# The MLP of a four-layer hybrid backbone: x spilled and fetched in pieces, the tenth pair's weights in the modulation buffers, the last modulation part in the layer's own MLP

## The reference

```python
m = silu(c) @ mod_w[i] + mod_b[i]            # six parts of 1024: m[0] to m[5]
...                                          # mixer with m[0], m[1], m[2]
h = rmsnorm(x, g4[2]) * (1.0 + m[4]) + m[3]
f = square(relu(h @ mlp_w1[i])) @ mlp_w2[i]  # 1024 -> 4096 -> 1024
x = x + m[5] * rmsnorm(f, g4[3])
```

## Time and profile before

| | us |
|---|---|
| median of 3 runs | 3561.32 (3553.54 to 3561.75) |
| the profiled execution | 3556.74 |
| its span | 3554.9 |
| PE busy | 3209.8 (90%) |
| PE weight load busy | 2971.0 (84%) |
| DVE busy | 2062.0 (58%) |
| POOL busy | 1944.1 (55%) |
| ACT busy | 1481.6 (42%) |
| mean granted TensorE clock | 0.961 of full |

### The profile page before, as it was taken

The page is one execution under the profiler, slowest core; times in us unless marked ns, Lnnn a source line. Parts: engine busy times, 40 slices in busy tenths (PEclk is TensorE's granted clock), DMA queues, the critical chain, the costliest instruction groups (busy, mean ns, idle before and its releaser), DMA issues.

```text
span 3554.9 us, 73409 instructions
## 1 busy us (share of the span) xinstructions
PE 3209.8 (90%) x28786; PEld 2971.0 (84%) x28786; DVE 2062.0 (58%) x3756; ACT 1481.6 (42%) x2812; POOL 1944.1 (55%) x1467
## 2 busy tenths in 40 slices
PE   5899998999999998898688889899988989999997
PEld 2789998899889997796577788899987856889996
DVE  8646884564558854859844444478735643543333
ACT  4344433422544444546432234444435343544442
POOL 0455676554556774525577744557764301556674
PEclk9899999999999998998799999999999999999999
DMA  7445553333355533336734433455533201342214
GB/s 283 160 148 186 199 196 136 121 118 101 114 195 183 185 121 122 124 120 219 234 102 118 114 80 108 143 201 178 184 113 101 91 17 36 115 159 84 89 55 155
DMA packets 210174, 489.63 MB, mean 138 GB/s; under 512 B 88576, under 2 KB 98368, under 8 KB 208064
## 3 DMA queue, kind: packets, MB, share of 16 engines
q1 hardware_dynamic: 179552, 444.59, 38.0%
q10 hardware_dynamic: 30304, 40.62, 3.3%
HBM read 432.29 MB, written 51.54 MB: 136 GB/s over the span
## 4 chain that ended last, share of the span: by engine, by line
issue 38%; PE 32%; POOL 12%; POOLq 10%; DVE 4%; DMA 1%; DVEq 1%; ACT 1%; ACTq 0%; SPq 0%
PE banks L1897 15%; POOL ws L844 10%; PE banks L1901 7%; POOLq L959 3%; PE banks L1059 3%; POOLq L956 3%; PE banks L1038 3%; PE banks L1069 2%; POOL wq L903 2%; PE banks L1043 1%; POOLq L870 1%; DMA wr<-in_w_slabs 1%; DVE mjunk L3127 1%; DVE mr L3127 1%; PE banks L1334 0%
## 5 line engine op out<-in xcount | busy, mean ns | idle before, releaser
L844 POOL TENSOR_TENSOR ws<-wr,ws 128x1024 fp32r<-128x1024 f32 x365 | 892.1, 2445 | 1199.9 <-ACT ws L2014 1199.3
L2014 ACT ACTIVATE ws<-wr 128x1024 fp32r<-128x1024 f32 x365 | 386.3, 1058 | 700.9 <-DMA wr<-in_w_slabs 379.2
L1059 PE MATMUL banks<-hs,ws 128*128 128x320 f32 (+2 forms) x2624 | 452.7, 324 | 62.3 <-DVE fs L3729 24.6
L1059 PEld LDWEIGHTS banks<-hs,ws 128*128 128x128 f32 x2624 | 411.0, 197 | 90.5 <-issue 49.3
L1059 PE MATMUL banks<-fs,ws 128*128 128x320 f32 x2304 | 386.6, 319 | 43.9 <-ACT ws L2014 28.1
L1059 PEld LDWEIGHTS banks<-fs,ws 128*128 128x128 f32 x2304 | 354.4, 193 | 64.8 <-ACT ws L2014 37.5
L1897 PE MATMUL banks<-fs,wq 128*128 128x320 f32 x2048 | 342.0, 309 | 0.0
L1897 PEld LDWEIGHTS banks<-fs,wq 128*128 128x128 f32 x2048 | 310.9, 188 | 0.1
L903 POOL TENSOR_TENSOR wq<-wr,wq 128x512 fp32r<-128x512 f32 x144 | 185.8, 1301 | 207.7 <-ACT wq L2762 206.4
L1069 PE MATMUL banks<-hs,ws 128*128 128x320 f32 (+2 forms) x1312 | 232.4, 319 | 2.6 <-POOL ws L844 2.6
L1897 PE MATMUL banks<-t,wq 128*128 128x320 f32 x1280 | 218.4, 314 | 0.0
(11 more groups left out here) (375 smaller groups left out, 6196.0 us busy)
## 6 DMA issues: line engine op xcount, KB each, us to landing
wr<-in_w_slabs SPq DMA_DIRECT2D x429, 512.0 KB, 3.7
mr<-in_m_slabs SPq DMA_DIRECT2D x183, 512.0 KB, 3.9
wp<-in_w_slabs SPq DMA_DIRECT2D x36, 1024.0 KB, 5.1
x_d<-x ACTq DMA_DIRECT2D x4, 2560.0 KB, 9.0
x<-x_d ACTq DMA_DIRECT2D x4, 2560.0 KB, 10.0
ar_d<-ar SPq DMA_DIRECT2D x16, 640.0 KB, 3.6
bk_d<-bt SPq DMA_DIRECT2D x16, 640.0 KB, 6.2
bk<-bk_d SPq DMA_DIRECT2D x16, 640.0 KB, 5.6
```

What stands on the lines that cost most here:

```text
L844: pool.tensor_tensor(ws[s % 2][:, 1, :], wr[:, s % 2, :], ws[s % 2][:, 0, :].bitcast(F32), ALU.subtract).then_inc(lo_ready, 1)
L1059: pe.matmul(pu[:, t % 2, h, 0:q - p], ws[s % 2][:, 0, k * P:(k + 1) * P], src[:, k, c, p:q], start=(k + c == 0), stop=False)
L2014: act.activation(ws[s % 2][:, 0, :], wr[:, s % 2, :], ACT.Copy).then_inc(hi_ready, 1)
```

## The change

- `mods_in_pair` now gives 5, 6, 6, 6, 5, 5, 5, 4 tiles for the eight pairs in every layer. The MLP of each layer does the last eight tiles of its own layer and the first 40 of the next; the coefficients of part 5 are made after pair 0. So layer 0 does 48 tiles and not 56, layers 1 and 2 stay at 48, layer 3 does 8, and also loads and copies silu(c).
- The tenth pair goes to two of the three mr buffers (after the last modulation tile is read), not to wr. Pair 8 waits for entry 7 of pair 7 like the others. When entry 10 of pair 7 is made, SP loads the first two output slabs into wr.
- x is stored in eight DMAs of 320 KB, one after ACT's part of each middle tile of half 0, and fetched in sixteen of 160 KB by SP (first the eight of half 0, then of half 1), each followed by the load of one output slab as far as there are any. DVE waits for the first eight before its first `add_pair`, and for the others at the end of `out_halves`.
- In the first stage of regular tiles the load of pair 0 and of one slab change their order with some modulation loads.
- ckv and kr are stored in layer 3's mixer-to-MLP stretch, not at the end.

```diff
--- before.py
+++ after.py
@@ -438,16 +438,16 @@
         part_copied, from_yp = yp_ready, KD
         u_taken, from_zeroed = yf_zeroed, 1
         s_made, from_tanh = tanh_ready, 2
-        x_moved, from_silu = silu_ready, 2
+        x_moved, from_silu, x_second, from_stored = silu_ready, 2, silu_stored, 16
         t_copied = sem("t_copied")
         t_made = sem("t_made")
 
         block = ctx.enter_context(nc.Block())
         mixers = {0: FFT_SLABS, 1: CONV_SLABS, 2: RWKV_SLABS, 3: MLA_SLABS}
 
-        def mods_in_pair(l):
-
-            return 6 if l == 0 else 5
+        def mods_in_pair(n):
+
+            return (5, 6, 6, 6, 5, 5, 5, 4)[n]
 
         def product_at(li, n, step):
 
@@ -553,13 +553,13 @@
 
                 p_mid, d = middles[li]
                 last = li == len(layers) - 1
-                tile = [-M_LEFT if li == 0 else 0]
+                tile = [-M_LEFT]
 
                 def load_mods(count):
 
                     for _ in range(count):
                         q = tile[0]
-                        if last or q == MTILES:
+                        if q == (0 if last else MTILES - M_LEFT):
                             return
                         j = q % MU
                         sp.wait_ge(mod_read[j], n[j])
@@ -571,11 +571,13 @@
 
                     if m == 0:
                         sp.wait_ge(t_made, 9 * li + 9)
-                    if m:
-                        sp.wait_ge(e_low, from_ahead + ENTRIES * li + entry_at(m - 1, 10 if m == PAIRS - 2 else 7) + 1
-                                   if m < PAIRS - 1 else from_ahead + ENTRIES * li + entry_at(PAIRS_U - 1, 10) + 1)
-                    to = wr if m == PAIRS - 1 else wp
-                    sp.dma_start(to[:, :, :], a["w_slabs"][d + 2 * m:d + 2 * m + 2].rearrange("s p n -> p s n")
+                    elif m < PAIRS - 1:
+                        sp.wait_ge(e_low, from_ahead + ENTRIES * li + entry_at(m - 1, 7) + 1)
+                    else:
+                        for j in range(2):
+                            sp.wait_ge(mod_read[j], n[j])
+                    to = mr[:, 0:2, :] if m == PAIRS - 1 else wp[:, :, :]
+                    sp.dma_start(to, a["w_slabs"][d + 2 * m:d + 2 * m + 2].rearrange("s p n -> p s n")
                                  ).then_inc(p_landed[m == PAIRS - 1], 16)
 
                 def load_u(i):
@@ -589,25 +591,38 @@
 
                 load_until(p_mid - KH + 2)
                 load_mods(3)
+                load_until(p_mid - 1)
                 load_pair(0)
-                load_until(p_mid - 1)
-                load_mods(2)
+                load_mods(1)
                 load_until(p_mid)
                 load_mods(2)
                 load_u(0)
-                load_mods(2)
+                load_mods(1)
                 load_u(1)
                 load_mods(2)
                 for m in range(PAIRS_U):
                     load_mods(2)
-                    load_pair(m + 1)
+                    if m < PAIRS - 2:
+                        load_pair(m + 1)
                     load_mods(1)
-                    for i in range(2):
-                        if m < PAIRS_U - 1:
-                            load_u(2 * m + 2 + i)
-                        load_mods(2 if i == 0 else mods_in_pair(li) - 5)
+                    if m < PAIRS_U - 1:
+                        load_u(2 * m + 2)
+                    load_mods(min(2, mods_in_pair(m) - 3))
+                    if m < PAIRS_U - 1:
+                        load_u(2 * m + 3)
+                    load_mods(mods_in_pair(m) - 5)
+                assert tile[0] == (0 if last else MTILES - M_LEFT)
                 load_pair(PAIRS - 1)
+                sp.wait_ge(e_low, from_ahead + ENTRIES * li + entry_at(PAIRS_U - 1, 10) + 1)
+                load_until(p_mid + 2)
                 sp.wait_ge(e_low, from_ahead + ENTRIES * (li + 1))
+                sp.wait_ge(product_done, product_at(li, PAIRS - 1, 7))
+                sp.wait_ge(x_moved, from_silu + 256 * li + 128)
+                for h in range(2):
+                    for k in range(KD):
+                        sp.dma_start(x[:, k, h * HT:(h + 1) * HT], x_d[:, k * T + h * HT:k * T + (h + 1) * HT]
+                                     ).then_inc(x_second if h else x_moved, 16)
+                        load_until(min(p_mid + 3 + KD * h + k, p_mid + 2 * KD))
 
             def load_const(name, t, landed):
                 sp.dma_start(t[tuple(slice(None) for _ in t.shape)], a[name]).then_inc(landed, 16)
@@ -817,10 +832,15 @@
                         load_m((q - M_AHEAD) // MU, q % MU)
                         load_until(at[0] + 1)
                 load_until(mixer_end + 2)
+                if l == 3:
+                    sp.wait_ge(ckv_ready, 1)
+                    sp.dma_start(a["ckv"], ckvo[:, :, :]).then_inc(x_stored, 16)
+                    sp.dma_start(a["kr"], kro[0:DR, :]).then_inc(x_stored, 16)
                 load_until(mixer_end + 3 * FB)
-                if not last:
-                    sp.wait_ge(silu_stored, 16)
-                    sp.dma_start(wp[:, :, :].rearrange("p g n -> p (g n)"), silu_d).then_inc(c_landed, 16)
+                if l == 3:
+                    sp.wait_ge(x_stored, 32)
+                sp.wait_ge(silu_stored, 16)
+                sp.dma_start(wp[:, :, :].rearrange("p g n -> p (g n)"), silu_d).then_inc(c_landed, 16)
                 load_until(mixer_end + 4 * FB)
                 load_middle(li, n)
                 start = mixer_end + MLP_STD
@@ -830,10 +850,6 @@
                     sp.wait_ge(x_ready, 4 * KD * len(layers) - 2 * KD + KD * h + k + 1)
                     c = slice(h * HT, (h + 1) * HT)
                     sp.dma_start(a["y"][k][:, c], x[:, k, c]).then_inc(x_stored, 16)
-            if 3 in layers:
-                sp.wait_ge(ckv_ready, 1)
-                sp.dma_start(a["ckv"], ckvo[:, :, :]).then_inc(x_stored, 16)
-                sp.dma_start(a["kr"], kro[0:DR, :]).then_inc(x_stored, 16)
             sp.wait_ge(x_stored, 16 * (2 * KD + 2 * (3 in layers)))
 
 
...
@@ -2261,7 +2277,7 @@
             def combine_high(k, li):
 
                 act.wait_ge(t_made, t_steps[0] + 1)
-                act.wait_ge(x_moved, from_silu + 32 * li + 16)
+                act.wait_ge(x_moved, from_silu + 256 * li + 128)
                 for to, value in ((t1[:, k, 0, :], sqx[:, 2, :]), (t34[:, k, 0, :], aux[:, 1, 0:HT]),
                                   (t2[:, k, 0, :], aux[:, 0, 0:HT]), (t34[:, KH + k, 0, :], aux[:, 2, 0:HT])):
                     op = act.activation(to, value, ACT.Copy)
@@ -2327,10 +2343,9 @@
                 for j in range(mid):
                     ahead()
                     round_two()
+                    act.dma_start(x_d[:, j * T:(j + 1) * T], x[:, j, :]).then_inc(x_moved, 16)
                 while done[0] < KD:
                     round_two()
-                if hidden:
-                    act.dma_start(x_d, x[:, :, :].rearrange("p k n -> p (k n)")).then_inc(x_moved, 16)
                 for j in range(n):
                     if j or mid:
                         ahead()
...
@@ -2842,7 +2857,6 @@
                     squared(n, 3)
                     if n < PAIRS - 1:
                         highs(n + 1, 3)
-                act.dma_start(x[:, :, :].rearrange("p k n -> p (k n)"), x_d).then_inc(x_moved, 16)
 
             def load(name, t, landed):
                 act.dma_start(t[tuple(slice(None) for _ in t.shape)], a[name]).then_inc(landed, 16)
@@ -3289,7 +3303,7 @@
                                       ).then_inc(f_ready, 1)
 
                 in_halves(CONV_SPLIT, 5, 0, 1, take)
-                coefficients(1, range(2, NMOD))
+                coefficients(1, range(2, 5))
                 m0 = CONV_SPLIT // 3
                 t0 = tile[0]
                 for m in range(m0, KD):
...
@@ -3755,15 +3769,13 @@
 
                     for _ in range(count):
                         q = mod_next[0]
-                        if last or q == MTILES:
+                        if q == (0 if last else MTILES - M_LEFT):
                             return
                         j = q % MU
                         mod_tile(mr[:, j, :], silu_near, bass.ds(q % MTILES, 1), m_landed[j], 16 * (used[j] + 1)
                                  ).then_inc(mod_read[j], 1)
                         used[j] += 1
                         mod_next[0] += 1
-                        if mod_next[0] == 0:
-                            coefficients(0, range(5, NMOD))
 
                 def pair_bank(n, i):
 
@@ -3825,17 +3837,17 @@
                     dve.tensor_tensor(to, pair_bank(n, b), to, ALU.add).then_inc(u_taken, 1)
 
                 in_halves(FB, 2, 3, 4, take, take_mid)
-                if not last:
-                    dve.drain()
-                    dve.wait_ge(c_landed, xc_in + 16 * (l + 1))
-                    dve.tensor_copy(silu_near[:, :, :], wp[:, :, :])
+                dve.drain()
+                dve.wait_ge(c_landed, xc_in + 16 * (l + 1))
```

(17 more changed lines are left out.)

8 lines of the change are left out of this document (4 added, 4 removed).

## The result

| | before | after |
|---|---|---|
| median, same chip | 3559.45 (3553.54 to 3561.75, 4 runs) | 3478.15 (3471.89 to 3480.02, 4 runs) |
| profiled execution | 3556.74 | 3471.89 |
| its span | 3554.9 | 3470.1 |
| mean granted TensorE clock | 0.961 | 0.969 |

The ratio is 0.9771, 95% interval 0.9753 to 0.9789. The forecast was 3497, a gain of 64; the medians differ by 81 and the two profiled executions by 85 (the changed kernel's is the fastest of its four). The direction and the range held; 17 us of gain by the medians, 21 by the profiled executions, were not in the sum.

What follows compares the result with a forecast made beforehand. PE is busy 90% of the span, so only its waits and slow matmuls can be won. -16.7 - 33.5 - 11.6 + 1 - 2 - 1 = -64 took the profiled 3556.7 to 3493, as a median 3497; range 3468 to 3535.

Steps and rivals of the forecast that it cites:

- Store in pieces: MLP's first half: eight stores of x remove 34.7 of PE stalls, 18 comes back, net -16.7.
- landing delay d: Extra landing time of a slab beside a 320 KB store piece, taken as 0.7; PE pays d/2 per tile.
- the loss of the lead: Second half of the MLP: the old stall gave the loader about 2.7 of lead; 1.7 a layer charged.
- Fetch in pieces, early slabs: Output tiles after pair 9: 43.5 of PE stalls go, 10 comes back, net -33.5.
- the slab loop's 1.6 a layer: Output tiles: loop of 7.3 against PE's 7.04 over 16 tiles costs 2.0, less 0.4 hidden by the norm's matmuls.
- Pair 8: Pairs 8 and 9: pair 8's weights load earlier, so POOL starts its sums sooner; 2.9 a layer, -11.6.
- Slab order at the regular tiles: Last regular tile: the slab loaded ahead of pair 0 may save 1 us that two layers lose, -2.
- Modulation moved: DVE's modulation tiles in the pairs: 0, covered by DVE's wait for PE; layer 3's new loads and copy +1.
- A: Rival: the spill and fetch pieces cost nothing, hidden by the slab loop; 3472, chance 0.15.
- B: Rival: every piece costs its full share, and POOL limits pairs 8 and 9; 3537, chance 0.2.
- C: Rival: slabs beside or behind a piece land 2.5 later in 24 tiles of a layer; slower, 3591, chance 0.05.
- D: Rival: output slabs still late, SP hanging on modulation reads of pair 7; no more than a share of B's chance.

Runs made afterwards that it cites:

- u_spill: The changed kernel with x stored in one DMA of 2560 KB again, after the middle tiles: 3492.74.
- relu_first: The changed kernel with ACT taking relu and square of a tile ahead of the high part of the slab two tiles on, in half 1: 3471.55.
- u_mods: The changed kernel with two modulation tiles again after the last regular tile, so four stand ahead of pair 0's c_sum add: 3491.9.
- no_store: The changed kernel with each of the eight stores of x cut to 8 columns, the fetch reading as many bytes from input x: 3470.9.
- u_fetch: The changed kernel with x fetched by SP in one DMA of 2560 KB, behind the first two output slabs: 3502.0.
- dve_sums: The changed kernel with the four block sums of pair 9 made by DVE instead of POOL: 3471.1.

## Why the prediction was right, and where it was not

- **Store in pieces:** forecast -16.7, measured -17.6 (u_spill 18.2). The sum is right and its parts are not, so that it came out near is in part luck. The landing delay d was right (0.6 for 0.7), but PE doesn't pay d/2 per tile: the pieces cost 5.0, where 8 x 0.35 x 4 = 11.2 stood. What was taken too low is "the loss of the lead": 1.7 a layer, of a lead of 2.7 for which no row stood. Of the 34.7, 17.1 came back; less the 5.0 that is 12, or 3 a layer, in half 1. Part of that is ACT's order: a late slab also holds back the relu, which relu_first shows.
- **Fetch in pieces, early slabs:** forecast -33.5 and -1 for the end, measured -38.8 (the end has 0.9 of it: from the last add to x to the end of the span 4.1 before, 3.2 after). The wait at the first tile came as forecast (0.87 for 0.8). The mis-sized term is the slab loop's 1.6 a layer over the output tiles: the tiles stand 3.52 apart, it cost nothing visible.
- **Pair 8:** forecast -11.6, measured -9.2. The prediction's own times (1297.6 less 1294.9) give 2.7 a layer where it took 2.9. Pair 8 came better than thought (26.5 for "27 to 28"), but POOL, which was noted as a bound only, then is the limit in pair 9 and takes 4.8 back.
- **Slab order at the regular tiles:** -2 forecast, -2.8 measured, by luck: the forecast laid it to the slab that now goes ahead of pair 0, and u_mods, which keeps that slab there, has all 2.8 again. What counted is how many modulation loads SP issues ahead of the next slab.
- **Modulation moved:** this step failed. It said 0, since "DVE waits 3.38 for PE in each pair". That holds in pairs 2 to 7, which changed by 0.0. But an edit that moves work also takes it away from where it stood, and the two tiles and the coefficients stood ahead of the first c_sum, where DVE had no wait at all. The rows of before showed it (0.16 "issue", 5.04 on PE) and I had read only a steady pair. It is 15.9 of the 21 that the forecast lacked against the profiled execution. Layer 3's new loads and copy cost nothing in its regular tiles and pairs (0 to 0.1), where 1 was taken; its middle tiles of half 0 grew by 1.7, more than those of the others (0.2 to 1.1), and no run tells whether the new loads have a part in that.

The rivals: A (the pieces cost nothing, 3472) was nearer in time than the forecast but by another cause; no_store shows that the stores cost 5. B (POOL eats the earlier pair, each piece its full share) has the right engine for pair 9 and the wrong size. C needed d = 1.9; it was 0.6. D did not occur: the early slabs are there.

## What to carry to other kernels

When work is moved, read the trace at the place that it leaves as closely as at the place to which it goes, and read the first round of a loop, not a steady one: an "issue" bracket of 0.16 on the instruction that PE waits for says that all that stands ahead of it on that engine is on the path. Cut a bulk transfer that runs beside a just-in-time loader into pieces between the loads; one of 2.5 MB, put back, cost 4.3 to 6.7 us a layer (u_spill, u_fetch), eight of 320 KB about 1.2, sixteen of 160 KB nothing that shows. And an engine that waits for a load should do the work that is already there first.

## What was not expected of the hardware

- DVE and POOL hold each other up in float32 adds with both inputs in SBUF. In dve_sums DVE took 1.47 to 1.61 for 128x512 beside POOL, in 15 of 16 adds, where the same shape with both inputs in SBUF takes it 0.69 while POOL is idle (after, 2764.96), and POOL's low parts took 3.00 and 3.23 for two instead of 2.54 and 2.56. The Trainium skill, SBUF — State Buffer, section Who interferes with whom, says that a DVE instruction with two inputs in SBUF contends with a POOL instruction that reads SBUF. By that rule, the trace agrees: both got longer. The 12 expected of dve_sums had not reckoned with it.
- A slab of 512 KB landed in 4.3 instead of 3.7 beside a 320 KB store, whether the store was in another queue or behind it in the same one; beside 160 KB fetches behind it in its own queue it landed in 3.6. Beside one store of 2560 KB (u_spill, 960 to 975) it took 8.3.
